# Sample values of a gated recurrence spread by DMA, and table products of a state-space layer in four row groups

## The chip, the cores and the metric

The kernel runs on one core of a Trainium2 chip. The metric is the device time of one execution in microseconds (us); the time before is the median of three runs. One further execution was profiled, and all rows come from it. Engines: TensorE (PE, its weight loads PEld), VectorE (DVE), ScalarE (ACT), GpSimd (POOL), SyncE (SP), which here only issues DMAs. All arithmetic is in 32-bit floats.

## The reference, cut to what matters

One step of a two-layer decoder trunk for a prompt of 512 tokens and 8 samples of one token each. Each layer is a half-step SwiGLU feed-forward block, a mixer, a cross-attention into 256 memory tokens and a second feed-forward block. Mixer 0 is S5, a diagonal complex state-space layer; mixer 1 is HGRN2, a gated recurrence with 8 heads and a 128x128 state per head. The change touches one piece of each.

For a sample, HGRN2 takes one step of the recurrence. Per head, with f, k, q and v vectors of 128:

```
S_new[k, v] = f[k] * S[k, v] + k_t[k] * v_t[v]        # 8 samples: 8 outer products
o[v]        = sum_k S_new[k, v] * q_t[k]
```

The kernel keeps channels on the 128 partitions: `k_t` of a sample is one column (a value per partition), which suits `f * S + k * v` with k on the partitions. But `v_t` also is a column, and the product needs it as a row that every partition can read.

For S5 the sequence is worked in blocks of 8 tokens. Tables hold the response of a group's 16 outputs to 16 inputs at 0 to 7 steps: products of `c * lambda^n` (`sGe` in the code) with `b` (`bZ`), summed over the 64 complex states of a group, plus the direct term `d` at step 0. They depend on the weights alone and are made on the chip at the start.

## The kernel before, in words

The trunk is a list of matrix products ("streams") over the same 520 token columns: for each pair of 128-column weight chunks, SP loads the chunk (`raw`), ScalarE rounds it (`w_hi`, L1329), VectorE takes the remainder (`w_lo`, L1826), and TensorE runs three products (`w_hi` with the high and low part of the activations, L3017, and `w_lo` with the high part, L3022). There are two `raw` buffers and two chunks (j = 0, 1) in a pair. SP issues a load when `lo_ready` says that VectorE has read the buffer's last content (L965). Each engine runs its own program in an order written out by hand; the engines meet in semaphores only.

S5 tables (during layer 0's first feed-forward block). GpSimd builds, for a = 0 to 7, the tables `sFe` and `sGe` of four pairs of groups (`table_part`, L736 to L738; `s5_tables` counts them). `sGe` has two buffers. At fixed places in its stream of products (`PREP`), TensorE's `prepare` runs two groups of transposes ("F") and then the group "K": for each of four pairs u, two products over bZ (real and imaginary part, 32 rows of output by 128 columns, L2565) and one of 16 columns with the identity (L2568). All four u write the PSUM partitions 0 to 31, at columns u*128. A 32-bit product is two instructions in the trace, a transpose one, so a "K" is 16 and 8 of them. ScalarE copies the bank to `sKst` (L1466) when the earlier table's copies have landed (`s5_k_out`), and SP writes it with 8 DMAs to memory (L945), each repeated over 8 steps. Places for a = 0 to 3 lie in `ffn1_out0` (one pair of chunks apart), for a = 4 to 7 in `ffn1_in1` (two pairs apart).

HGRN2 (`hg_in`, 16 pairs, two per head). The iteration h runs four weight chunks (forget gate, queries, values, output gate), and between them small groups for head g = h - 1 (attention inside chunks of 64 tokens, the state's increments "D", the outputs "O") and e = h - 2 (the samples' outputs "S" and "T", the norm "N", "R"). `HG` lists the groups in order; group q uses PSUM bank q mod 4, and TensorE waits for the bank's earlier content to be read (`reuse`). After "D" come two groups "B": TensorE transposes each sample's value column, repeated over 128 columns, against the identity (8 transposes per head, L2818), so that every partition holds the row v. VectorE reads it from PSUM: 8 instructions `sS = vrow * k + sS` (L2315), four per bank, after ScalarE has multiplied sS by f (L1703). VectorE's order in an iteration ends: values into `hgV` (L2187), the prompt's states (L2205), the samples' states (L2315), the split of the next pair's chunk 0 (L1826), two products (L2326, L2327), the output gate (L2329). SP loads the samples' states (L921, after the odd pair's loads), and stores those of head h - 2 (L908, L910, after the even pair's loads, from the fifth pair on). The weights of the next stream, `hg_out`, are requested by SP when the 16 pairs of `hg_in` are through; TensorE starts on them in iteration 8 (`projected`, L2896).

## Time and profile before

| what | value |
|---|---|
| median of 3 runs | 2366.99 us (2365.1 to 2368.97) |
| profiled execution, its own time | 2364.88 us |
| profiled execution, span | 2363.1 us |
| TensorE busy | 2341.2 us (99%) |
| VectorE, ScalarE, GpSimd busy | 1292.9, 871.4, 608.2 us |
| memory traffic | 289 MB, 122 GB/s on average |

The span is from the first to the last instruction; the execution's own time is 1.8 us more. Busy time of TensorE is the union of its matmuls, whose ends are modelled and overlap, so the cost of a group is best read as the distance from its start to the next group's start. A timeline row gives the start in us, the length, engine, line, operation, output and inputs, how many instructions are merged, and in brackets the idle time before it with its releaser.

### The profile page before, as it was taken

How to read it: one execution, taken by the hardware profiler on the slowest of the kernel's cores; microseconds unless marked ns; L12 is line 12 of the kernel's file. 1: busy time of each engine (PE TensorE's matmuls, PEld its weight loads, DVE VectorE, ACT ScalarE, POOL GpSimd, SP SyncE). 2: the span in 40 equal slices, each digit the busy share in tenths (PEclk: the TensorE clock that was granted, in tenths of full speed). 3: DMA queues.
4: the chain of work that ended last, by engine and by line, in shares of the span. 5: the costliest groups of instructions: out<-in, count | busy, mean ns of one | idle time of the engine just before them, and what ended most of it. 6: DMA issues, size and time to landing. Idle time of an engine off the chain costs nothing.

```text
span 2363.1 us, 50146 instructions
## 1 busy us (share of the span) xinstructions
PE 2341.2 (99%) x21043; PEld 2280.2 (96%) x21043; DVE 1292.9 (55%) x1906; ACT 871.4 (37%) x1399; POOL 608.2 (26%) x591
## 2 busy tenths in 40 slices
PE   8999999999999999999999999999999999999999
PEld 8999999889979999999999999999999979999999
DVE  6653643864576543445543344577778666443443
ACT  4422333543233231232333233267775233321323
POOL 4779958331103000004121010432222102000003
PEclk9999999999999999999999999999999999999999
DMA  6456445563463333333543333333332653333332
GB/s 169 128 156 151 119 123 156 182 184 107 148 242 101 95 91 91 98 104 87 169 119 106 105 104 116 86 99 103 109 104 81 214 188 90 98 94 94 98 93 95
DMA packets 483707, 289.19 MB, mean 122 GB/s; under 512 B 22289, under 2 KB 466962, under 8 KB 482514
## 3 DMA queue, kind: packets, MB, share of 16 engines
q1 hardware_dynamic: 477856, 280.66, 40.3%
q0 software_dynamic: 560, 1.84, 0.6%
q10 hardware_dynamic: 5122, 4.25, 0.5%
q8 instruction: 129, 2.11, 0.4%
q14 instruction: 40, 0.33, 0.0%
HBM read 258.86 MB, written 27.85 MB: 121 GB/s over the span
## 4 chain that ended last, share of the span: by engine, by line
PE 89%; DVE 4%; POOL 3%; ACT 2%; DMA 1%; issue 1%; SPq 0%; DVEq 0%; POOLq 0%; ACTq 0%
PE lin L3017 50%; PE lin L3022 25%; PE mis L2511 3%; POOL sTmp L737 1%; PE mis L2648 1%; PE mis L2631 1%; POOL sGe L738 1%; PE lin L2598 1%; POOL sGe L736 1%; PE lin L2979 1%; POOL sFe L738 1%; PE lin L2648 0%; DMA raw<-in_xattn_w_kv_dram 0%; PE lin L2760 0%; DVE w_lo L1826 0%
## 5 line engine op out<-in xcount | busy, mean ns | idle before, releaser
L1826 DVE TENSOR_TENSOR w_lo<-raw,w_hi 128x1024 fp32r<-128x1024 f32 (+1 forms) x322 | 463.4, 1439 | 297.7 <-ACT w_hi L1329 297.1
L1329 ACT ACTIVATE w_hi<-raw 128x1024 fp32r<-128x1024 f32 (+1 forms) x328 | 364.9, 1113 | 305.7 <-PE lin L3022 251.3
L3017 PE MATMUL lin<-a_rear,w_hi 128*128 128x264 f32 x3552 | 455.5, 279 | 0.0
L3017 PE MATMUL lin<-a_front,w_hi 128*128 128x256 f32 x3552 | 451.5, 279 | 1.1 <-DVE a_rear L1839 0.7
L3017 PEld LDWEIGHTS lin<-a_rear,w_hi 128*128 128x128 f32 x3552 | 432.6, 188 | 0.0
L3017 PEld LDWEIGHTS lin<-a_front,w_hi 128*128 128x128 f32 x3552 | 424.4, 188 | 4.6 <-issue 1.9
L3022 PE MATMUL lin<-a_rear,w_lo 128*128 128x264 f32 x1776 | 245.2, 278 | 0.0
L3022 PE MATMUL lin<-a_front,w_lo 128*128 128x256 f32 x1776 | 240.5, 277 | 0.9 <-DVE w_lo L1826 0.9
L2390 DVE SCALAR_TENSOR_TENSOR xT<-lin,xT 128x520 f32<-128x520 f32 (+1 forms) x87 | 60.8, 699 | 322.2 <-PE lin L3022 321.5
L1062 POOL TENSOR_TENSOR acc<-xT 128x520 f32<-128x520 f32 x8 | 12.2, 1520 | 864.0 <-DVE xT L2390 835.9
L3022 PEld LDWEIGHTS lin<-a_rear,w_lo 128*128 128x128 f32 x1776 | 223.8, 188 | 0.0
L3022 PEld LDWEIGHTS lin<-a_front,w_lo 128*128 128x128 f32 x1776 | 219.5, 188 | 1.6 <-DVE w_lo L1826 1.5
L1740 ACT ACTIVATE f_front<-t 128x256 fp32r<-128x256 f32 (+1 forms) x88 | 36.9, 419 | 395.1 <-DVE t L2371 395.1
L3017 PE MATMUL lin<-f_rear,w_hi 128*128 128x264 f32 x1386 | 178.1, 281 | 0.0
L3017 PEld LDWEIGHTS lin<-f_rear,w_hi 128*128 128x128 f32 x1386 | 170.5, 188 | 0.1
L3017 PE MATMUL lin<-f_front,w_hi 128*128 128x256 f32 x1386 | 170.3, 276 | 0.0
L3017 PEld LDWEIGHTS lin<-f_front,w_hi 128*128 128x128 f32 x1386 | 163.3, 188 | 0.1
L1736 ACT ACTIVATE t<-t 128x520 f32<-128x520 f32 x88 | 56.5, 642 | 278.6 <-DVE t L2365 278.6
L2369 DVE TENSOR_TENSOR t<-lin,rstd 128x520 f32<-128x520 f32 x88 | 61.5, 699 | 158.5 <-PE lin L3022 158.4
L1066 POOL TENSOR_TENSOR sqt<-xT 128x520 f32 (+1 forms) x54 | 81.9, 1517 | 211.0 <-DVE xT L2390 148.9
L3017 PE MATMUL lin<-g_all,w_hi 128*128 128x264 f32 (+1 forms) x1024 | 128.8, 278 | 0.0
L3017 PEld LDWEIGHTS lin<-g_all,w_hi 128*128 128x128 f32 x1024 | 122.8, 188 | 1.1 <-DVE g_all L1966 1.1
(512 smaller groups left out, 3207.9 us busy)
## 6 DMA issues: line engine op xcount, KB each, us to landing
raw<-in_ffn_w_in_dram SPq DMA_DIRECT2D x176, 512.0 KB, 3.9
raw<-in_ffn_w_out_dram SPq DMA_DIRECT2D x64, 704.0 KB, 4.6
kc<-in_cache_mem_k_dram SPq DMA_DIRECT2D x32, 512.0 KB, 7.0
vc<-in_cache_mem_v_dram SPq DMA_DIRECT2D x16, 1024.0 KB, 9.4
raw<-in_hg_w_in_dram SPq DMA_DIRECT2D x32, 512.0 KB, 4.3
raw<-in_xattn_w_kv_dram SPq DMA_DIRECT2D x16, 512.0 KB, 4.4
raw<-in_s_w_glu_dram SPq DMA_DIRECT2D x16, 512.0 KB, 4.1
raw<-in_xattn_w_q_dram SPq DMA_DIRECT2D x16, 512.0 KB, 3.9
```

The costliest lines, as they stand in the source:

```text
L736: link(eng.tensor_tensor(out[:, e], pv[0], mv[e], ALU.mult))
L738: link(eng.tensor_tensor(out[:, e], out[:, e], tmp, sign))
L1066: step.link(pool.tensor_tensor(sqt[:], tile(xT, m), tile(xT, m), ALU.mult))
L1329: act.activation(w_hi[:, j, 0:kt, :], raw[:, j, 0:kt, :], ACT.Copy).then_inc(hi_ready, 1)
L1736: act.activation(t2[:], t1[:], ACT.Silu).then_inc(gate_out, 1)
L1740: ins = act.activation(tile(out, i), t3[:, cols], ACT.Copy)
L1826: dve.tensor_tensor(low_weights(n, j), raw[:, j, 0:kt, :], w_hi[:, j, 0:kt, :].bitcast(F32), ALU.subtract).then_inc(lo_ready, 1)
L2369: step.link(dve.tensor_tensor(t4[:], lflat(1), rstd[:], ALU.mult))
L2390: dve.scalar_tensor_tensor(out=tile(xT, m), in0=lflat(j), scalar=scale, in1=tile(xT, m), op0=ALU.mult, op1=ALU.add)\
L2511: ins = pe.matmul(kv_bank(c)[:, 0:NM], w[:, e, k, :], x[:, k, :], start=k == 0 and u == 0, stop=k == KD - 1 and u == 2)
L3017: pe.matmul(lpart(j, half), high[:, k, :], (x_lo if u else x_hi)[half][:, k, :], start=start and u == 0 and k == 0, stop=False)
L3022: ins = pe.matmul(lpart(j, half), low[:, k, :], x_hi[half][:, k, :], start=False, stop=k == kt - 1)
```

## The change

"B" goes. TensorE's 16 groups (64 transposes) are left out of `HG` and of its program. In their place SP writes the head's 8 value columns from `hgV` to a small tensor in memory (`values_out`; the order is turned, so the pieces are 4 bytes, 1024 of them) and, in a second DMA, reads the 8 rows back into all 128 partitions (`values_spread`, 4 KB per partition, 512 KB in all) into `vB`, which has two buffers. VectorE takes the row from `vB` in SBUF instead of PSUM and waits for `spread_in`. A semaphore `sampled` takes the place of the old bank counters. In SP's program, with i the pair, `values_out(i // 2 - 1)` stands after the even pair's loads and `values_spread(i // 2 - 1)` after the odd pair's `sample_states_in`. `values_out` of the last head stands behind the loop, ahead of the first load of `hg_out`; its spread stands between the first pair's two loads.

"K" is packed. The four u write the PSUM partitions 32u to 32u+31, columns 0 to 127, with the loop over real and imaginary part outside; the four identity products follow. ScalarE then copies 128x128 instead of 32x512, and SP takes the rows from there.

```diff
+    vB = [at(f"vB{e}", [P, NS, P], F32, (o_hid + 6 * HTILE, o_tmp + 5 * TILE)[e]) for e in range(2)]
+    hg_v = nc.dram_tensor("hg_v", (HH, NS, P), F32, kind="Internal").ap()
...
-    sKst = at("sKst", [2 * SC, 4, P], F32, o_s0 + 31360)
+    sKst = at("sKst", [P, P], F32, o_s0 + 31360)
...
-            made += [("D", (g, 0), "dve"), ("D", (g, 1), "dve"), ("B", (g, 0), "dve"), ("B", (g, 1), "dve")]
+            made += [("D", (g, 0), "dve"), ("D", (g, 1), "dve")]
...
-                HG.emptied_of(sp, "B", (h, 1))
+                sp.wait_ge(sampled, h + 1)
                 sp.dma_start(o_["hg_s"][0, :, h].rearrange("b k v -> k b v"), sS[h % 2][:]).then_inc(hg["s_out"], 16)
+
+            def values_out(h):
+                sp.wait_ge(used[0], first_pair["hg_in", 1] + 2 * h + 2)
+                sp.dma_start(hg_v[h].rearrange("b v -> v b"), hgV[h % 2][:, SEQ:NT],
+                             allow_slow_non_contiguous=True).then_inc(spread_out, 16)
+
+            def values_spread(h):
+                sp.wait_ge(spread_out, 16 * (h + 1))
+                if h >= 2:
+                    sp.wait_ge(sampled, h - 1)
+                    sp.wait_ge(spread_in, 16 * h)
+                src = bass.AP(tensor=hg_v.tensor, offset=h * NS * P, ap=[[0, P], [P, NS], [1, P]])
+                sp.dma_start(vB[h % 2][:], src).then_inc(spread_in, 16)
...
-                            sp.dma_start(dst, sKst[SC * g:SC * (g + 1), u:u + 1, :].to_broadcast([SC, CS, P]))\
+                            r0 = 2 * SC * u + SC * g
+                            sp.dma_start(dst, sKst[r0:r0 + SC, :].unsqueeze(1).to_broadcast([SC, CS, P]))\
...
+                        if first and j == 0 and ST[n][0] == "hg_out":
+                            values_spread(HH - 1)
...
                         if i % 2:
                             sample_states_in(i // 2)
-                        elif i >= 4:
-                            states(i // 2 - 2)
+                            if i >= 3:
+                                values_spread(i // 2 - 1)
+                        elif i >= 2:
+                            values_out(i // 2 - 1)
+                            if i >= 4:
+                                states(i // 2 - 2)
+                    values_out(HH - 1)
...
-                        act.activation(sKst[:], bank[0:2 * SC, :].rearrange("p (j n) -> p j n", j=4), ACT.Copy)\
+                        act.activation(sKst[:], bank[:, 0:P], ACT.Copy)\
...
                 def values(p, b):
                     dve.wait_ge(chunk_done, 2 * p + 3)
+                    if p >= p0 + 4:
+                        dve.wait_ge(spread_out, 16 * ((p - p0) // 2 - 1))
...
+                        dve.wait_ge(spread_in, 16 * (g + 1))
                         for f in range(2):
-                            q = G.at("B", (g, f))
                             dve.wait_ge(hg["s_decay"], 2 * g + f + 1)
-                            dve.wait_ge(hg["fill"], q + 1)
                             for u in range(4):
                                 s_ = 4 * f + u
                                 ins = dve.scalar_tensor_tensor(
-                                    out=sS[g % 2][:, s_], in0=hg_bank(q)[:, u * P:(u + 1) * P],
+                                    out=sS[g % 2][:, s_], in0=vB[g % 2][:, s_],
                                     scalar=hgK[g % 2][:, SEQ + s_:SEQ + s_ + 1], in1=sS[g % 2][:, s_],
                                     op0=ALU.mult, op1=ALU.add)
-                            ins.then_inc(hg["void_dve"], 1)
+                        ins.then_inc(sampled, 1)
...
+                        rows = [slice(2 * SC * u, 2 * SC * (u + 1)) for u in range(4)]
+                        for e in range(2):
+                            for u in range(4):
+                                pe.matmul(bank[rows[u], 0:P], bZ[:, e, 4 * a + u, :, :].rearrange("p g c -> p (g c)"),
+                                          sGe[a % 2][:, e, u, 0:CS, :], start=e == 0, stop=False, skip_group_check=True)
                         for u in range(4):
-                            for e in range(2):
-                                pe.matmul(bank[0:2 * SC, u * P:(u + 1) * P],
-                                          bZ[:, e, 4 * a + u, :, :].rearrange("p g c -> p (g c)"),
-                                          sGe[a % 2][:, e, u, 0:CS, :], start=e == 0, stop=False)
-                            ins = pe.matmul(bank[0:2 * SC, u * P:u * P + SC], ident[:, 2 * SC * u:2 * SC * (u + 1)],
-                                            dD[:, a, :], start=False, stop=True)
+                            ins = pe.matmul(bank[rows[u], 0:SC], ident[:, rows[u]], dD[:, a, :], start=False, stop=True,
+                                            skip_group_check=True)
...
-                elif what == "B":
-                    h, f = a
-                    for u in range(4):
-                        b = SEQ + 4 * f + u
-                        ins = pe.transpose(bank[:, u * P:(u + 1) * P], hgV[h % 2][:, b:b + 1].to_broadcast([P, P]), ident[:])
...
                         hg_increments(g)
-                        hg_group("B", (g, 0))
-                        hg_group("B", (g, 1))
```

Left out of the diff: the semaphores' declarations, and three waits on "B" (ScalarE before it overwrites `hgK`, TensorE before "S", SP above) that now name `sampled`.

## Rows read from the trace of the kernel before

**Rows 1.** The page: busy us and share; TensorE's granted clock in 40 slices.

```profile
PE 2341.2 (99%) x21043; PEld 2280.2 (96%) x21043; DVE 1292.9 (55%) x1906; ACT 871.4 (37%) x1399; POOL 608.2 (26%) x591
...
PEclk9999999999999999999999999999999999999999
```

**Rows 2.** Stretches, one head: length, busy PE, PEld, DVE, ACT, POOL, clock, DMA share, GB/s.

```profile
1649.00:1681.00 32.00, 32.00 (x368) 30.41 (x367) 24.34 (x50) 23.58 (x39) 7.59 (x8) 1.00 0.37 102
```

**Rows 3.** Timeline of TensorE, first table group: start, duration, what.

```profile
157.70 0.62 PE L2565 MATMUL mis<-sGe,bZ 128*32 128x128 f32 x4
158.16 0.21 PE L2568 MATMUL mis<-dD,ident 128*32 128x16 f32 x2
...
159.80 2.39 PE L3017 MATMUL lin<-f_rear,w_hi 128*128 128x264 f32 x18
```

**Rows 4.** The same view of TensorE, a steady head.

```profile
1635.27 0.64 PE L2784 MATMUL mis<-sS,hgQ 128*32 128x128 f32 x16
1635.84 0.66 PE L2798 MATMUL mis<-ident,hgV 128*128 128x128 f32 x4
...
1652.22 1.09 PE L2818 MATMUL mis<-ident,hgV 128*128 128x128 f32 x8
1653.07 2.13 PE L3017 MATMUL lin<-a_front,w_hi 128*128 128x256 f32 x16
```

**Rows 5.** Timeline of GpSimd, ends of the third, fourth and fifth table.

```profile
192.80 1.43 POOL L738 TENSOR_TENSOR sGe<-sGe,sTmp 128x576 f32<-128x576 f32 x1
...
212.00 1.41 POOL L738 TENSOR_TENSOR sGe<-sGe,sTmp 128x576 f32<-128x576 f32 x1
...
231.34 2.29 POOL L738 TENSOR_TENSOR sGe<-sGe,sTmp 128x576 f32<-128x576 f32 x1
```

**Rows 6.** Timeline of TensorE at the third, fourth and fifth table.

```profile
194.56 0.62 PE L2565 MATMUL mis<-sGe,bZ 128*32 128x128 f32 x4
...
213.60 0.60 PE L2565 MATMUL mis<-sGe,bZ 128*32 128x128 f32 x4 [0.54 <-POOLq L1190]
...
239.11 0.62 PE L2565 MATMUL mis<-sGe,bZ 128*32 128x128 f32 x4
```

**Rows 7.** Timeline of VectorE: two products and a sample update.

```profile
1569.01 1.23 DVE L2326 TENSOR_TENSOR dgQ<-dgQ,hgQ 128x512 f32<-128x512 f32 x1 [0.62 <-ACT dgQ L1696]
...
1657.45 2.15 DVE L2315 SCALAR_TENSOR_TENSOR sS<-mis,hgK,sS 128x128 f32<-128x128 f32 x8
...
1660.66 0.68 DVE L2326 TENSOR_TENSOR dgQ<-dgQ,hgQ 128x512 f32<-128x512 f32 x1
```

**Rows 8.** Timeline of TensorE in the second head's span.

```profile
1599.25 0.97 PE L3022 MATMUL lin<-a_front,w_lo 128*128 128x256 f32 x6 [0.45 <-DVE w_lo L1826]
```

**Rows 9.** Timeline of SyncE's queue at the end of the stage.

```profile
1770.22 10.53 SPq L965 DMA_DIRECT2D raw<-in_hg_w_out_dram  x2
```

**Rows 10.** Timeline of VectorE there.

```profile
1782.11 0.69 DVE L2187 TENSOR_TENSOR hgV<-lin,rstd 128x520 f32<-128x520 f32 x1
...
1787.72 1.22 DVE L1826 TENSOR_TENSOR w_lo<-raw,w_hi 128x1024 fp32r<-128x1024 f32 x1
...
1801.87 2.06 DVE L2315 SCALAR_TENSOR_TENSOR sS<-mis,hgK,sS 128x128 f32<-128x128 f32 x8
```

**Rows 11.** Timeline of ScalarE there.

```profile
1784.99 1.05 ACT L1329 ACTIVATE w_hi<-raw 128x1024 fp32r<-128x1024 f32 x1
```

**Rows 12.** Timeline of TensorE there.

```profile
1789.77 0.39 PE L2896 MATMUL lin<-h_hi,w_hi 128*128 128x256 f32 x1
...
1791.75 0.65 PE L2784 MATMUL mis<-sS,hgQ 128*32 128x128 f32 x16 [0.28 <-ACT hO L1718]
...
1804.04 0.72 PE L2874 MATMUL mis<-rT,ident 64*128 64x130 f32 x8 [0.15 <-DVE sS L2315]
```

**Rows 13.** The page's DMA issues: pieces' tile, KB each, median us to landing.

```profile
raw<-in_hg_w_out_dram SPq DMA_DIRECT2D x8, 512.0 KB, 3.8
...
bRaw<-in_s_b_re_dram SPq DMA_DIRECT2D x2, 128.0 KB, 5.4
```

More of the change, by code:

```diff
@@ L453, in trunk_kernel @@
            "scaled_dve", "front", "state_out", "s_decay", "s_out", "squares", "inverse")}
-    rows_in = [sem(f"rows_in{b}") for b in range(NS)]
+    rows_in = [sem(f"rows_in{b}") for b in range(4)]
+    spread_out, spread_in, sampled = sem("spread_out"), sem("spread_in"), sem("sampled")
     consts_done = sem("consts_done")
@@ L1646, in hg_in @@
                         if h >= 2:
-                            G.emptied_of(act, "B", (h - 2, 1))
+                            act.wait_ge(sampled, h - 1)
                             act.wait_ge(hg["scaled_pool"], POOLS * (h - 1))
@@ L2780, in hg_group @@
                 if what == "S":
-                    G.emptied_of(pe, "B", (a, 1))
+                    pe.wait_ge(sampled, a + 1)
                     for b in range(NS):
```

## The prediction

> **What bounds the kernel now.** I read the page first. TensorE is busy for 2341.2 of 2363.1 us and its clock is granted in full in all 40 slices, so the upper of the two levels throughout [rows 1]. No other engine is above 55%. So the span is TensorE's program, with some 22 us of gaps, and what leaves TensorE's program shortens the span unless another engine is late at the next meeting. Then I read the two stages that the change touches. In a steady head of the HGRN stage TensorE works 32.00 of 32.00 us, VectorE 24.34, ScalarE 23.58 [rows 2]. In the table stage TensorE's groups stand close behind GpSimd's tables: the fourth "K" is the one place where TensorE waits for them, 0.54 us [rows 6].
>
> **K packed.** Before, a group lasts from 157.70 to 159.80, 2.10 us; one u has a quarter, 0.525 us; its two small instructions start 0.46 us after its four large ones, so a large one costs 0.115 us and a small one (0.525 - 0.46)/2 = 0.03 us [rows 3]. How the packed form runs is shown by the "S" groups: the same shape (128 rows, 32 columns of weights, 128 moving columns) in turns over four sets of output partitions, and 16 instructions from 1635.27 to 1635.84, 0.036 us each [rows 4]. So a new K is 16 x 0.036 + 8 x 0.036 = 0.86 us, and saves 1.24 us. The bounds: nothing, if only "S" overlaps for a reason of its own, and 2.10 - 0.57 = 1.53 us if the small ones hide. I take 1.24, from the nearest row.
>
> The Trainium skill (TensorE: Matmul & The Clock Gate, "The mechanism") states that a weight load overlaps running matmuls only when it is for other rows of the array; here all groups use all 128 rows, so by that rule the packed K would save nothing. The "S" rows, also on 128 rows, speak against it; what it would give is the second rival.
>
> How many of the eight count? GpSimd's third and fourth sGe end at 194.23 and 213.41; TensorE takes them at 194.56 and 213.60 [rows 5, 6]. GpSimd works without regard to when TensorE is done. When the first two K save 2.48 us, TensorE stands at the third at 192.08 and waits until 194.4; the fourth starts at 213.6 as before. So the savings of the first three are all given back as waits, and only the fourth's own 1.24 us is left. The fifth table ends at 233.63 and is used at 239.11, 5.5 us of slack; that place is 25.5 us behind the fourth's, the later ones as far apart again, where a table takes 20 us [rows 5, 6], so the last four save in full (a wait of ScalarE for the earlier copies' landing stands in the same stretch and moves with them). K: 5 x 1.24 = 6.2 us. The smaller copy on ScalarE is off the path.
>
> **B removed.** From the start of "B" to the next chunk is 1653.07 - 1652.22 = 0.85 us, 6.8 us over eight heads [rows 4]. In the five middle heads (g = 1 to 5) nothing is late behind it: the chunk of weights between hides VectorE's work, and both helpers are idle for some 8 us in 32 [rows 2]. They save 4.25 us. The first head (g = 0) saves nothing: TensorE already waits 0.45 us for a split that stands behind the sample update in VectorE's program [rows 8], and comes 0.85 us earlier to the same wait. For the last two see below.
>
> **What VectorE pays.** An update takes 2.06 to 2.15 us for eight, 0.26 us each, from PSUM [rows 7, 10]. From SBUF both inputs share a memory with GpSimd's work. A product of 512 columns takes 0.68 us alone and 1.23 us beside GpSimd [rows 7], so the streaming part of 0.13 us of a 128-column one can double; against that the read from PSUM goes. I take +0.3 us for eight with GpSimd at work (bounds: -0.5 and, with all of it doubled, +2.1). It counts only in the first head, where the split is waited for: -0.3 us. In middle heads it is hidden.
>
> **The DMAs.** The spread of head g is issued behind the sample states' load, which waits for the end of "S" at 1635.84 [rows 4], so at about 1636.5; 512 KB land in 3.8 us alone [rows 13], at most some 9 us behind the states' load. VectorE wants them at 1657.45 [rows 7]: over 10 us of slack. The turned store is 1024 pieces of 4 bytes, 64 per DMA engine. The trace has no such store. Nearest is bRaw: 2048 pieces of 64 bytes landing in 5.4 us behind another load [rows 13], hence at most 0.04 us per piece and engine. I take 0.01 to 0.04 us, 1 to 3 us for all 64 and landing in 2 to 4 us; as bounds nothing and 0.2 us a piece. The DMAs are busy for 0.37 of a head [rows 2] and SP has pauses where the two stand.
>
> The Trainium skill (DMA: Bandwidth & Descriptors, "Rules for kernel authors") states that a copy whose last dimension isn't contiguous becomes one descriptor per element, and the same page, "Specifications", that pieces below 512 bytes cost a read-modify-write. No row here shows what that makes of a 4-byte store; its effect would be the fourth rival.
>
> **The end of the stage is where the change costs.** SP requested `hg_out`'s first chunk at 1770.22 and its second ten us later [rows 9]. Now `values_out(7)` stands ahead of them and waits for hgV of head 7, which ends at 1782.80 [rows 10]. So the first load starts at 1783.35 instead of 1770.22 and lands after 3.8 us [rows 13], at 1787.15; ScalarE, which split it at 1784.99 [rows 11], now does so from 1787.2 to 1788.25, and VectorE's split, before from 1787.72 to 1788.94 [rows 10], ends at 1789.5. TensorE's first product of `hg_out` was at 1789.77 [rows 12]; without B it would be there at 1788.9 and waits until 1789.55. Behind the split stand the output gate and ScalarE's copy of "O", for which TensorE already waits at 1791.75 [rows 12]; that meeting moves by the split's delay, 0.57 us. So the seventh head's saving (g = 6) is gone, and 0.6 us are lost. The second load must wait for the store's landing, about 1785, and arrives near 1790.2, ahead of its use, which follows the copies of "O" at 1792 [rows 12]. With the store at its 4 us both shift and the loss is 2 to 4 us. In the last head (g = 7) TensorE waits in "R" for a bank that the update frees [rows 12]; now "R" takes a bank that is free, but "S" behind it needs the update, which ends at 1803.93 [rows 10] against 1803.8 for TensorE: some 0.6 of the 0.85 us stay.
>
> **Sum.** 6.2 + 4.25 - 0.3 - 0.6 + 0.6 = 10.15 us. The profiled execution's own time is 1.8 us above its span: 2364.9 - 10.15 = 2354.7 us. The median shown stands 2.1 us above that execution: 2366.99 - 10.15 = 2356.8 us. The likeliest case's own range is 2354 to 2360 (updates at +0.3 or below, store of 1 to 3 us).
>
> **Rivals.**
> 1. GpSimd doesn't hold TensorE. If its tables came sooner, for instance because the freed TensorE or VectorE gets out of its way, all eight K count: 3 x 1.24 = 3.7 us more, and the two ends of HGRN without loss another 2.5: 2366.99 - 16.4 = 2350.6 us. Against it: its table ends are set by its own unbroken work [rows 5].
> 2. The packed K runs no faster: 2366.99 - 3.95 = 2363.0 us. For it only that weights and moving columns differ from "S" in content; against it the 0.036 us [rows 4].
> 3. HGRN gives nothing: store at 4 us and update at +1 us, so 3 us at the end and 1 us in the first head against 4.25 + 0.6: 2366.99 - 6.2 - 0.85 = 2359.9 us, or up to 2362 if ScalarE's long wait moves too.
> 4. Slower, by SP's queue: the 4-byte pieces take 0.2 us each. Then the 64 of an engine last 12.8 us, `hg_out`'s first chunk lands at 1786.2 + 12.8 = 1799.0, 12.4 us late for VectorE; in six middle heads the next weights arrive about 1.8 us after they are wanted, 10.8 us. Against 10.8 us saved elsewhere that is 12.4 us slower: 2379.4 us. It decides from about 0.17 us a piece. For it: no row shows such a store, and waits of SP and VectorE now hang on it. Against it: 64-byte pieces at 0.04 us or less [rows 13].
>
> **How the numbers follow.** A difference counts above 0.2% (4.7 us), about what this kernel's measurement can tell from none; so faster means below 2362.3. Chances: forecast 0.55, rival 1 0.08, rival 2 0.12, rival 3 0.17, rival 4 0.08. Faster: 0.55 + 0.08 + 0.14 of rival 3 + 0.02 of rival 2 = 0.79; slower 0.08; same 0.13. The range leaves out rival 4 and most of rival 1 and reaches over rival 2: 2352.5 to 2364.0.
>
> **What would show it.** Right: L2565 in about 0.6 us a group of 16, next chunk 0.86 us after its start; TensorE's wait on GpSimd up from 0.5 to about 4 us in two waits; no L2818; about 31.2 us a head; `hg_out`'s first load some 13 us after its old place in the head and a wait of TensorE near its first product. Wrong: a K still near 2 us (rival 2); the third and fourth K without waits (rival 1); L2315 above 3 us, or VectorE waiting for `spread_in` (3, 4); landings of the 4-byte store above 5 us. The forecast as a whole is wrong if TensorE's gaps grow by more than what left its program.

## The result, and the profile after

The changed kernel takes 2375.68 us, median of 11 runs (2371.62 to 2376.94), against 2367.34 us for 11 runs of the kernel before on the same chips. The ratio is 1.0033, 95% interval 1.0025 to 1.0041: about 8 us slower, where 10 us less were forecast and 2364.0 was the range's end. The profiled execution took 2376.84 us, its span is 2375.1 us.

The page of the changed kernel, the lines that answer to [rows 1]:

```profile
PE 2335.1 (98%) x20979; PEld 2271.5 (96%) x20979; DVE 1305.3 (55%) x1906; ACT 870.4 (37%) x1399; POOL 605.0 (25%) x591
...
PEclk9999999999999999999999999999998999999999
```

TensorE's work fell by only 6.1 us, and its gaps grew from 22 to 40 us: by the prediction's last sentence that alone makes it wrong. One slice of the clock is no longer full. The list of TensorE's waits in the changed kernel (line waited at, releaser: total us, times, longest) says where:

```profile
PE lin L2920 <- DVE w_lo L1853: 11.0, 1, 11.0
...
PE lin L3044 <- DVE w_lo L1853: 3.8, 4, 2.9
PE mis L2594 <- POOLq L1217: 3.0, 2, 2.8
...
PE mis L2839 <- ACT vTok L1663: 1.7, 1, 1.7
```

**The stage's end.** The queue of SyncE, then ScalarE, VectorE and TensorE in the changed kernel, the answer to [rows 9 to 12]:

```profile
1782.41 0.37 SPq L919 DMA_DIRECT2D hg_v<-hgV  x1
1782.83 0.57 SPq L985 DMA_DIRECT2D raw<-in_hg_w_out_dram  x1
1792.69 0.33 SPq L929 DMA_DIRECT2D vB<-hg_v  x1
...
1797.05 1.06 ACT L1356 ACTIVATE w_hi<-raw 128x1024 fp32r<-128x1024 f32 x1 [12.39 <-DMA raw<-in_hg_w_out_dram]
...
1787.75 0.72 PE L2898 MATMUL mis<-rT,ident 64*128 64x130 f32 x8
1799.42 0.58 PE L2920 MATMUL lin<-h_hi,w_hi 128*128 128x256 f32 x1 [10.96 <-DVE w_lo L1853]
1799.80 0.41 PE L2920 MATMUL lin<-h_lo,w_hi 128*128 128x256 f32 x1
1800.01 0.41 PE L2920 MATMUL lin<-h_hi,w_lo 128*128 128x256 f32 x1
...
1802.32 1.08 PE L2813 MATMUL mis<-sS,hgQ 128*32 128x128 f32 x16
```

The store of 4-byte pieces is requested at 1782.41; the spread, which waits for nothing but its landing, follows at 1792.69, 10.3 us later. The load of weights behind it is in memory 14.2 us after its request, where such a load took 3.8 [rows 13]. And once TensorE has stood for 11 us, its products start 0.21 us apart instead of 0.12, and "S" takes 1.08 us instead of 0.65 [rows 12]: the lower of the two clock levels. The view by stretches (length, busy PE, PEld, DVE, ACT, POOL, granted clock, DMA share, GB/s) shows how long that lasts:

```profile
1799.40:1805.40 6.00, 5.98 (x40) 5.00 (x41) 4.38 (x7) 3.18 (x8) 0.00 (x0) 0.50 0.39 113
1800.00:1820.00 20.00, 18.89 (x246) 16.24 (x246) 14.11 (x35) 11.55 (x25) 0.00 (x0) 0.86 0.19 55
```

A granted clock of 0.50 is the lower level throughout: some 6 us of work at half speed, so about 3 us lost.

The slow store doesn't show as busy DMA engines. The DMA view of the stretch from 1782 to 1784.8 counts the packets; two rows of the view by stretches follow:

```profile
DMA packets 1072, 0.02 MB, mean 7 GB/s; under 512 B 1040, under 2 KB 1072, under 8 KB 1072
...
1784.80:1786.80 2.00, 2.00 (x27) 1.80 (x25) 1.91 (x4) 0.00 (x0) 2.00 (x2) 1.00 0.00 0
1786.80:1792.60 5.80, 1.66 (x38) 1.40 (x36) 1.90 (x7) 0.00 (x0) 0.18 (x1) 0.94 0.33 29
```

All 1024 pieces have started by 1784.8. For the next 2 us nothing moves, and up to the landing the load behind them trickles at 29 GB/s. What the time between the last piece's start and the landing goes into isn't shown.

**The second head.** It answers to [rows 8], where TensorE waited 0.45 us. SyncE, ScalarE, VectorE and TensorE of the changed kernel:

```profile
1561.47 0.37 SPq L919 DMA_DIRECT2D hg_v<-hgV  x1
1564.62 6.30 SPq L985 DMA_DIRECT2D raw<-in_hg_w_in_dram  x2
...
1576.95 1.06 ACT L1356 ACTIVATE w_hi<-raw 128x1024 fp32r<-128x1024 f32 x1 [6.62 <-DMA raw<-in_hg_w_in_dram]
...
1595.05 4.63 DVE L2343 SCALAR_TENSOR_TENSOR sS<-vB,hgK,sS 128x128 f32<-128x128 f32 x8
...
1578.55 0.66 PE L2839 MATMUL mis<-lvl 128*64 128x32 f32 x16 [1.75 <-ACT vTok L1663]
...
1579.65 3.30 PE L3039 MATMUL lin<-a_front,w_hi 128*128 128x256 f32 x16
...
1600.86 2.08 PE L3044 MATMUL lin<-a_front,w_lo 128*128 128x256 f32 x8 [2.89 <-DVE w_lo L1853]
```

Two things are late here: ScalarE's split of weights whose load stands behind the first head's store, with the copy vTok behind it; and VectorE's w_lo, behind an update of 4.63 us where it was 2.15 [rows 7]. After each wait a run of 16 products that takes 2.1 us takes 3.3, or eight take 2.08 instead of 1.07.

**K.** The first packed group, and the third, in the changed kernel, the answer to [rows 3, 6]:

```profile
159.44 0.64 PE L2594 MATMUL mis<-sGe,bZ 128*32 128x128 f32 x16
...
160.06 1.12 PE L3039 MATMUL lin<-f_rear,w_hi 128*128 128x264 f32 x7
...
196.33 0.65 PE L2594 MATMUL mis<-sGe,bZ 128*32 128x128 f32 x16 [2.84 <-POOLq L1217]
...
196.95 4.47 PE L3039 MATMUL lin<-f_rear,w_hi 128*128 128x264 f32 x22
```

A group costs 0.62 us, not 2.10. The wait on GpSimd's third table is the forecast one; the 22 products behind it take 4.47 us where such a run takes 2.78 elsewhere: again the lower clock, 1.7 us. That fall costs nothing in the end, because the fourth table isn't there any earlier. In a second profile of K packed alone (k_only_again) the clock stayed up, and TensorE waited for the fourth table instead:

```profile
194.56 0.64 PE L2567 MATMUL mis<-sGe,bZ 128*32 128x128 f32 x16 [2.85 <-POOLq L1191]
...
195.19 2.87 PE L3019 MATMUL lin<-f_rear,w_hi 128*128 128x264 f32 x22
...
213.73 0.64 PE L2567 MATMUL mis<-sGe,bZ 128*32 128x128 f32 x16 [2.14 <-POOLq L1191]
```

The wait there is 2.14 us; in the changed kernel it is 0.15.

For the comparisons below the HGRN stage is measured between events that every kernel has: VectorE's hgV of the first, third and eighth head, and the request of the first load of the stage after `hg_out`. From TensorE's first K group to the first scan product of the state-space stage is K's part. All in us, from one profiled execution each; the row of before is first:

| kernel | first K | K to scan | hgV 1 to 3 | hgV 3 to 8 | hgV 8 to end | HGRN sum |
|---|---|---|---|---|---|---|
| before | 157.70 | 267.88 | 57.52 | 161.23 | 54.50 | 273.25 |
| changed | 159.44 | 262.65 | 63.38 | 157.57 | 66.20 | 287.15 |
| k_only | 159.20 | 262.00 | 57.54 | 161.24 | 54.49 | 273.27 |
| hg_only | 162.61 | 267.85 | 63.63 | 159.35 | 65.32 | 288.30 |
| load_first | 160.11 | 262.08 | 64.46 | 157.61 | 55.10 | 277.17 |
| pieces32 | 159.42 | 261.91 | 62.25 | 160.61 | 56.61 | 279.47 |
| before_sbuf | 157.87 | 267.98 | 59.24 | 161.75 | 55.83 | 276.82 |
| no_transfers_k | 158.51 | 263.89 | 60.73 | 157.84 | 55.24 | 273.81 |
| k_late | 159.70 | 262.03 | 57.49 | 161.24 | 54.49 | 273.22 |
| mixed | 157.90 | 260.56 | 57.48 | 158.72 | 55.59 | 271.79 |
| mixed_again | 161.11 | 260.43 | 57.51 | 158.72 | 55.67 | 271.89 |
| k_only_again | 157.64 | 260.55 | 57.49 | 161.23 | 54.49 | 273.21 |
| mixed25 | 159.93 | 260.46 | 57.48 | 158.91 | 54.50 | 270.89 |

The opening scatters: the first K group stands anywhere from 157.6 to 162.6, which is why medians and not single spans are compared. The HGRN columns repeat to 0.1 us (mixed and mixed_again, k_only and k_only_again).

"K to scan" has two levels among the ten profiles with packed groups: 260.4 to 260.6 us in mixed, mixed_again, mixed25 and k_only_again, and 261.9 to 263.9 in the other six. In those six the clock fell around 416 us, just before the scan, for 3.4 us (no_transfers_k: 6.8), and in the four it didn't. k_only and k_only_again are the same program, so this is scatter between executions. A row of k_only, then the same stretch of k_only_again:

```profile
414.00:421.00 7.00, 6.55 (x52) 6.02 (x50) 5.42 (x10) 3.44 (x12) 2.36 (x1) 0.76 0.33 86
...
414.00:421.00 7.00, 7.00 (x120) 6.81 (x122) 5.99 (x12) 3.57 (x11) 1.03 (x1) 1.00 0.74 213
```

What makes it fall there isn't shown: TensorE's waits just before, 0.9 and 0.45 us, are the same in before, where it stays up (1.00 in this stretch).

### The profile page after: what moved, and what is told of

Its sections match the earlier page's. It is cut to its first block, busy times and chain, and to the rows that moved or that the text cites. A ratio compares the mean times of both kernels' runs of the same rounds, so it can differ in the third digit from the quotient of the medians.

```text
span 2375.1 us, 50038 instructions
## 1 busy us (share of the span) xinstructions
PE 2335.1 (98%) x20979; PEld 2271.5 (96%) x20979; DVE 1305.3 (55%) x1906; ACT 870.4 (37%) x1399; POOL 605.0 (25%) x591
## 4 chain that ended last, share of the span: by engine, by line
PE 70%; DVE 6%; ACT 3%; DMA 2%; issue 1%; POOL 0%; DVEq 0%; SPq 0%; ACTq 0%; POOLq 0%
PE lin L3039 40%; PE lin L3044 20%; PE mis L2539 3%; DVE sS L2343 1%; PE mis L2677 1%; PE mis L2660 1%; DVE w_lo L1853 1%; DMA raw<-in_hg_w_out_dram 1%; DVE hS L2234 1%; DMA raw<-in_hg_w_in_dram 1%; PE lin L2677 0%; DMA raw<-in_xattn_w_kv_dram 0%; PE lin L2789 0%; ACT w_hi L1356 0%; PE lin L2920 0%
```

## The experiments

**1. K alone (k_only).** The kernel before with the four edits of the K groups: the shape of `sKst`, the source rows of its stores, ScalarE's copy and the order of the products.

```
-    sKst = at("sKst", [2 * SC, 4, P], F32, o_s0 + 31360)
+    sKst = at("sKst", [P, P], F32, o_s0 + 31360)
...
+                                pe.matmul(bank[rows[u], 0:P], bZ[:, e, 4 * a + u, :, :]...
```

> The kernel before with the packed K groups alone; HGRN keeps its B transposes. Theory 1 (the loss is all HGRN's: the store of 4-byte pieces holds up the SyncE queue, and TensorE, once idle, works at the lower clock for some us; K packed keeps its gain): 0.62 us a group instead of 2.10 saves 1.48 each, 11.8 over eight, of which about 3 go into waits on GpSimd's tables at the third and fourth group and 1.5 to 2 into products at the lower clock behind the third: 4 to 7 us faster than before (about 2362). Rival A (packing K is what fails: the wait at the third table and the clock fall cost as much as the eight groups gain): within 1 us of before.

Measured: 2359.8 us, ratio 0.9968 (0.9956 to 0.998), 7.3 us faster, just above the 4 to 7 expected. Rival A is out. Its HGRN stage is that of before to 0.02 us.

**2. HGRN alone (hg_only).** All the other edits of the change, K groups as before.

> The kernel before with HGRN's two transfers alone; K groups as before. Theory 1: the wait of 11 us at the stage's end with 3 us of slow products behind it, and some 5 to 6 us in the second head, less about 0.6 us a head in five heads: 11 to 15 us slower than before. Rival A: 7 to 9 us slower, the whole of the change's loss. Rival B (the loss comes from VectorE's slower update of sS, whose operands now all lie in SBUF): the same total, but with waits of TensorE on VectorE in every head.

Measured: 2384.63 us, ratio 1.0072 (1.0058 to 1.0086), 17.5 us slower, beyond what was expected. The HGRN stage accounts for 15.05 us of it (in the profiled execution the opening was 4.9 us longer as well). The two halves of the change (-7.3 and +17.5) add up to the +8 within their intervals. Rival B's waits in every head aren't there: between the third and eighth hgV it is faster than before (159.35 and not 157.6, for one gap of 1.4 us that no wait explains).

**3. The load ahead of the store (load_first).**

```
-                        if first and j == 0 and ST[n][0] == "hg_out":
+                        if first and j == 1 and ST[n][0] == "hg_out":
+                            values_out(HH - 1)
                             values_spread(HH - 1)
...
-                    values_out(HH - 1)
                     return
```

> The changed kernel, with hg_out's first two weight loads issued ahead of the last head's store and spread; nothing else moved. Theory 1: hg_out's first load is in memory in time, TensorE's 11 us wait at 1799 and the slow products behind it go (about 13 us): 2361 to 2365 us, faster than before by 2 to 6; the last head's sample update comes later, but has the first hg_out chunks to hide in. Rival B: only the queue's part goes and VectorE still holds TensorE: 2366 to 2370.

Measured: 2365.68 us, ratio 0.9993 (0.9983 to 1.0002): 10 us less than the changed kernel, between theory 1's 2365 and rival B's 2366. The profile decides between them. The first `hg_out` product in this kernel, and the store and spread:

```profile
1784.30 0.37 SPq L919 DMA_DIRECT2D hg_v<-hgV  x1
1795.46 0.34 SPq L929 DMA_DIRECT2D vB<-hg_v  x1
...
1791.79 0.38 PE L2920 MATMUL lin<-h_hi,w_hi 128*128 128x256 f32 x1 [1.44 <-DVE w_lo L1853]
1792.01 0.28 PE L2920 MATMUL lin<-h_lo,w_hi 128*128 128x256 f32 x1
```

The store still takes 11 us, but nothing waits for it. The wait of 10.96 is 1.44, the products come 0.12 apart, and the last stretch falls from 66.20 to 55.10. So it is the load's place behind the slow store, the order on SyncE's queue, that cost 11 us. The 0.6 us that remain at the end and the 6.9 in the first heads have other causes (experiments 5 and 6).

**4. Pieces of 32 bytes (pieces32).** The changed kernel; DRAM holds the values as [v][b], and VectorE strides.

```
-                sp.dma_start(hg_v[h].rearrange("b v -> v b"), hgV[h % 2][:, SEQ:NT],
-                             allow_slow_non_contiguous=True).then_inc(spread_out, 16)
+                sp.dma_start(hg_v[h], hgV[h % 2][:, SEQ:NT]).then_inc(spread_out, 16)
...
-                                    out=sS[g % 2][:, s_], in0=vB[g % 2][:, s_],
+                                    out=sS[g % 2][:, s_], in0=vB[g % 2][:, :, s_],
```

> The changed kernel, but the eight sample values of a partition are stored as one piece of 32 bytes (128 pieces instead of 1024), the spread stays one contiguous read of 4096 bytes per partition, and VectorE reads its values with a stride of 32 bytes. The order on the SyncE queue is that of the change. Theory 1 (price per piece, about 0.15 us for each of 64 on a DMA engine): the store lands 2 to 3 us after its issue instead of 10, and hg_out's first load 4 to 7 us instead of 14: 2360 to 2365 us, and the second head's wait goes too. Rival C (the price is the write through memory itself or its order in the queue, not the number of pieces): the store still lands 8 to 10 us after issue and the time stays at 2374 to 2377. Strided reads on VectorE: none of the theories needs them slower; if they are, the update takes over 4 us for eight in every head.

Measured: 2367.64 us, ratio 0.9998 (0.9989 to 1.0007). The queue of SyncE, and VectorE in a steady head:

```profile
1783.58 0.34 SPq L919 DMA_DIRECT2D hg_v<-hgV  x1
1783.97 0.43 SPq L984 DMA_DIRECT2D raw<-in_hg_w_out_dram  x1
1784.99 0.32 SPq L928 DMA_DIRECT2D vB<-hg_v  x1
...
1658.32 4.07 DVE L2342 SCALAR_TENSOR_TENSOR sS<-vB,hgK,sS 128x128 f32<-128x128 f32 x8
```

The same 4 KB, through the same memory and in the same place of the queue, have landed after 1.4 us as 128 pieces (8 per DMA engine) and after 10.3 us as 1024 (64): (10.3 - 1.4)/56 = 0.16 us a piece and engine. This is a quotient of landing times; by the packets above no engine is seen to work 0.16 us on a piece. Rival C is out, and the wait on vTok is gone too. The edit also changes which pieces lie side by side in memory (neighbouring 4-byte pieces of the turned store come from different partitions); that this, and not the count, makes the store slow was not tested. The total missed its forecast: the strided read makes the update 4.07 instead of 3.45 us, a steady head lasts 32.0 us as before the change, and TensorE still waits 3.49 us for w_lo in the second head and 1.97 at the first `hg_out` product. What removing B and packing K give is eaten by VectorE.

**5. Only the operand's place (before_sbuf).** The kernel before; VectorE reads the identity tile instead of the bank, TensorE still makes B.

```
-                                    out=sS[g % 2][:, s_], in0=hg_bank(q)[:, u * P:(u + 1) * P],
+                                    out=sS[g % 2][:, s_], in0=ident[:],
```

> The kernel before, whose only edit is that VectorE's sS update reads the identity tile in SBUF instead of the sample values in PSUM (the new states are wrong by that; TensorE still makes and VectorE still awaits the B groups, no transfer is added). It tells what makes an update of eight take 3.5 us in the steady heads and 4.6 us in the first instead of 2.15. Theory 2 (an operation with both tile operands in SBUF is slower while GpSimd works): 3.4 to 3.5 us in the steady heads, over 4 in the first, 2.1 in the last head where GpSimd is idle, and TensorE waits about 3 us on w_lo in the second head: 3 to 5 us slower than before. Rival D (the new transfers' traffic makes it slower): 2.15 us everywhere, time as before.

Measured: 2371.45 us, ratio 1.0009 (1.0 to 1.0018), 3.0 us slower by the medians, and an HGRN stage 3.6 us longer. TensorE waits 2.08 us for w_lo in the second head, not the 3 expected. VectorE in a steady head and in the last head of this kernel:

```profile
1660.35 3.51 DVE L2315 SCALAR_TENSOR_TENSOR sS<-ident,hgK,sS 128x128 f32<-128x128 f32 x8
...
1806.63 2.09 DVE L2315 SCALAR_TENSOR_TENSOR sS<-ident,hgK,sS 128x128 f32<-128x128 f32 x8
```

No transfer is added here, so rival D is out: the operand's place alone takes the update from 2.15 to 3.51, and in the last head, where GpSimd is idle, it costs nothing. The way it happens shows in the changed kernel. Windows narrow enough to hold a single update, beside GpSimd's last two operations of that head:

```profile
1659.62 0.60 DVE L2343 SCALAR_TENSOR_TENSOR sS<-vB,hgK,sS 128x128 f32<-128x128 f32 x1
1660.15 1.35 DVE L2343 SCALAR_TENSOR_TENSOR sS<-vB,hgK,sS 128x128 f32<-128x128 f32 x1
...
1658.80 1.28 POOL L1322 TENSOR_TENSOR outK<-outK,hgK 128x512 f32<-128x512 f32 x1
1660.04 1.31 POOL L1324 TENSOR_TENSOR inQ<-inQ,hgQ 128x512 f32<-128x512 f32 x1
```

The group is not slower evenly. Six of the eight updates take their usual 0.34 us (starting 0.26 apart). The first begins while GpSimd's outK operation is under way and ends 0.15 us after it (1660.22 against 1660.07); the second begins 0.11 us into the next operation and ends 0.15 us after that one. The first two are held for 0.26 and 1.01 us, together the 1.3. The first head has three such holds, 0.39, 1.03 and 1.03 us, and so its group costs 2.5 us more:

```profile
1595.05 0.73 DVE L2343 SCALAR_TENSOR_TENSOR sS<-vB,hgK,sS 128x128 f32<-128x128 f32 x1
1595.70 1.37 DVE L2343 SCALAR_TENSOR_TENSOR sS<-vB,hgK,sS 128x128 f32<-128x128 f32 x1
1596.99 1.37 DVE L2343 SCALAR_TENSOR_TENSOR sS<-vB,hgK,sS 128x128 f32<-128x128 f32 x1
...
1594.88 0.75 POOL L1320 TENSOR_TENSOR lvl<-lvl,hgK 128x256 f32<-128x256 f32 x1
1595.56 1.36 POOL L1322 TENSOR_TENSOR outK<-outK,hgK 128x512 f32<-128x512 f32 x1
1596.88 1.34 POOL L1324 TENSOR_TENSOR inQ<-inQ,hgQ 128x512 f32<-128x512 f32 x1
```

The Trainium skill (SBUF — State Buffer, "Who interferes with whom") states that a VectorE instruction with two SBUF inputs and a GpSimd instruction that reads SBUF exclude each other, the later one blocked until the first is done. The trace agrees, 1.35 us against 1.31. It agrees without exception: in the profile of the changed kernel 15 of the 64 updates begin during a GpSimd operation, and each of them ends 0.15 us after it; the other 49 take at most 0.35 us.

**6. B removed, no transfers (no_transfers_k).** The changed kernel without store, spread and their waits; the update reads the identity tile.

```
-                            if i >= 3:
-                                values_spread(i // 2 - 1)
...
-                    values_out(HH - 1)
...
-                        dve.wait_ge(spread_in, 16 * (g + 1))
```

> The changed kernel without its two transfers: nothing is stored or spread, nobody waits for them, and the sS update reads the identity tile in SBUF (the new states are wrong by that). It shows what the removal of B is worth when the transfers cost nothing. By theory 2 a steady head is 31.4 us as in the changed kernel (not shorter), the second head's wait on w_lo stays, the waits at vTok and at the stage's end go: 2359 to 2362 us. Rival D: the w_lo wait goes as well, 2354 to 2357.

Measured: 2362.43 us, ratio 0.9977 (0.9967 to 0.9987), a stage of 273.81 us: even with free transfers, removing B and reading the row from SBUF makes the stage 0.56 us longer. Rival D is out here too. What makes this kernel faster than before is K packed. The steady stretch gains 3.4 us (161.23 to 157.84); the first heads lose 3.2, the end 0.7. TensorE in the second head of this kernel:

```profile
1597.97 1.69 PE L3034 MATMUL lin<-a_front,w_lo 128*128 128x256 f32 x8 [3.05 <-DVE w_lo L1846]
1599.46 3.19 PE L3029 MATMUL lin<-a_rear,w_hi 128*128 128x264 f32 x16
```

The transfers themselves cost nothing in steady heads (157.57 with them), 2.7 to 3.7 us in the first, and 11 at the end.

**7. K packed from the fourth group on (k_late).**

```
+K_LATE = 3
...
+                        for e in range(2) if a >= K_LATE else ():
```

> The kernel before with K packed for the fourth to eighth group alone. If the first three packed groups only win time that GpSimd's third table and the lower clock behind that wait take back (3 x 1.48 = 4.4 us won, 2.8 waited, about 1.7 at the lower clock), this is as fast as all eight packed: 2359 to 2361 us, and TensorE has no wait over 1 us before 400. Rival E (the wait is not paid for by the first three groups, or the clock's fall costs nothing): all eight packed stay ahead of it by over 1.5 us.

Measured: 2360.74 us, ratio 0.9966 (0.9954 to 0.9978), and 262.03 us from the first K group to the scan, against 262.00 with all eight packed (k_only; the clock fell around 416 us in both, so they compare). The first three packed groups are worth nothing, as the prediction had it. But for the input at the opening, no single wait before the scan is above 0.9 us.

**8. Spread only where it pays (mixed, mixed_again, mixed25).** All K groups packed; the heads outside the list keep B.

```
+SPREAD = list(range(2, 7))        # mixed; range(2, 6) in mixed25
...
+            if g not in SPREAD:
+                made += [("B", (g, 0), "dve"), ("B", (g, 1), "dve")]
```

> All K groups packed; HGRN's values spread by the two transfers only for the third to seventh of the eight heads, the first two and the last keep their B transposes. By theories 1 and 2 it has the 0.64 us of each steady head (5 heads, 3.2 us) without the second head's waits and without the store ahead of hg_out's first load: 3 us faster than K packed alone, 2355 to 2358. Rival F (the transfers cost as much in the steady heads as B): no faster than K packed alone, 2359 to 2361.

Measured: 2362.46 us (2356.17 to 2366.62), ratio 0.9978 (0.9969 to 0.9987), slower than expected (2355 to 2358) though its stage is 1.5 us shorter than k_only's. So it was repeated beside k_only, with mixed25:

> The mixed version again, beside K packed alone on the same chip: its median was 2362.5 where its profiled execution gave 2356. If that is the scatter of the opening (TensorE's first table group stood between 157.7 and 162.6 us in the profiles so far, whatever the kernel), the median is 2358 to 2362 and the stage's length again 271.8 +- 0.3. If the transfers disturb in some executions, the stage of this profile is over 1 us longer.

> K packed alone, again, as the mate of the two mixed versions: 2359 to 2361 us, stage 273.3 us.

> As the mixed version, but with the transfers only for the third to sixth head (4 heads; the first two and the last two keep B). In the mixed version the stage was 1.5 us shorter than with all B groups, and not 3.2: the seventh head's update (3.5 us) delays w_lo for hg_out's first chunk (TensorE waits 1.43) and hO (1.05 instead of 0.28), 1.9 us more than before. Theory 2: with B in the seventh head both waits go back to those of before, the stage is 4 x 0.64 = 2.6 us shorter than 273.3 (270.7), and the time 2 to 3 us under K packed alone: 2357 to 2358. Rival F: the stage is no shorter than 271.8 and the time within 1 us of K packed alone.

Measured: mixed_again 2360.25 us (0.9954 to 0.9978), k_only_again 2360.17 (0.9948 to 0.9975), mixed25 2357.95 (0.9943 to 0.997). The run mixed_again is thus no faster than k_only_again, though its stage is 1.3 us shorter; its opening was 3.5 us later (161.11 against 157.64 in the profiles). mixed25 lies within what was expected of it. The stage of mixed25 is 270.89 us, 2.4 shorter than before, and its `hg_out` products are reached without the wait on w_lo. With the seventh head's row from SBUF (mixed) the same place showed 1.43 us of waiting, and it did so in no_transfers_k, where nothing is stored: that wait is VectorE's longer update. TensorE there in mixed25, the answer to the middle one of [rows 12]:

```profile
1783.35 0.64 PE L2836 MATMUL mis<-sS,hgQ 128*32 128x128 f32 x16 [0.25 <-ACT hO L1760]
```

mixed25 is the fastest of all, 11 us (0.43%) under the kernel before. Its lead of 2.2 us over K packed alone is what its stage shows, but within the scatter of the medians; by the runs' times alone it isn't settled.

## Why the prediction was wrong, step by step

- **K packed** held. The group saves 1.48 us, not 1.24, near the upper bound of 1.53: the large instructions cost 0.029 us each and the small ones about 0.02, not 0.036. The savings of the first three are given back, and k_late shows it by itself. In k_only_again they are given back as waits of 2.85 and 2.14 us; in the changed kernel as 2.84 and 0.15 and 1.7 at the lower clock between the two. What had no term is the other fall of the clock, around 416 us, in six of the ten profiles with packed groups: "K to scan" is 7.3 us shorter than before without it (5 x 1.48 = 7.4) and 4.0 to 6.0 with it. Measured for K alone -7.3 us against -6.2. Rival 2 is out, and so is the rule of the Trainium skill behind it (TensorE: Matmul & The Clock Gate, "The mechanism"): K packed runs as "S" does, although each group uses all rows of the array.
- **B removed** was mis-sized: 3.4 us over five steady heads in no_transfers_k, 0.68 each, where 0.85 was taken. "Nothing is late behind it" was wrong by 0.24 us in each of the last four (32.05 us a head became 31.44); 0.10 to 0.16 of it shows as TensorE's wait for the bank that VectorE's hO empties behind the longer update.
- **What VectorE pays** failed. Taken: +0.3 us for eight, one head. Measured: +1.3 in a steady head and +2.5 in the first, where it counts in full; the second figure is outside even the bound of +2.1. The error is the model: I let the streaming part double, and the measured form is that an update which begins during a GpSimd operation stands still until that is over. With the clock's fall behind it, the first heads lose 3.2 us without any transfer (57.52 to 60.73), where the prediction counted 0.3.
- **The DMAs** failed on the size. Taken: 0.01 to 0.04 us a piece, landing in 2 to 4 us. Measured: 0.16, landing in 10.3. The nearest row, 64-byte pieces, was no guide to 4-byte ones. The Trainium skill's rule of one descriptor per element (DMA: Bandwidth & Descriptors, "Rules for kernel authors") would have made the count of pieces the thing to fear. Its rule on pieces below 512 bytes (the same page, "Specifications") doesn't tell these cases apart, since 32-byte pieces landed in 1.4 us.
- **The end of the stage** had the right mechanism and the wrong size. The load did start 12.6 us later than [rows 9], and everything named behind it was late; but the last stretch grew by 11.7 us (54.50 to 66.20), where the sum had -0.6 for the end and +0.6 for the last head. It follows from the step before: the load's delay by a slow store, plus some 3 us of products at the lower clock. Of the 11.7, 0.7 come without any store, from the held update of the seventh head (55.24 in no_transfers_k).
- **The sum** of the profiled pair: K -5.2, first heads +5.9, steady heads -3.7, end +11.7, opening +1.7, all else +1.6, together +12.0 us of span. The medians differ by 8.3: the profiled execution of before lies 2.5 us under its median (its opening, 157.70, is one of the shortest), that of the changed kernel 1.2 above.
- **Rival 4** (chance 0.08) named the cause at the end and was close in its price, 0.2 us a piece for 0.16. It said that it decides from 0.17, so it was short where the other two costs were missing, and its 10.8 us in the middle heads didn't come: those heads aren't hurt by the transfers at all. That its total of 2379.4 us lies only 3.7 from the measured 2375.68 is in part luck: the 10.8 us were missing, and the loss in the first heads and at the lower clock wasn't in it.

Left open: why the stretch between the scan and the HGRN stage was up to 2 us longer than before in some profiles, with the transfers (hg_only, load_first) and without them (before_sbuf, k_only_again); why the clock falls around 416 us in some executions; and what holds the 4-byte store after its last piece has started.

## What to carry to other kernels

Before a transposing store goes on a queue, count its pieces per DMA engine and look at what stands behind it; move the next load ahead of it, or write whole short rows. Replacing a PSUM operand by one in SBUF isn't free on VectorE: look at what GpSimd does at that moment, and add what is left of each of its operations that an update meets, not a share of it. Where the bounding engine comes to stand for some us, add the slow products behind the wait to the price of the wait, unless its next wait takes them in; and apply a change that works in the steady state to the steady state alone.

## What the runs showed of the hardware

- A store of 64 pieces of 4 bytes per DMA engine has landed after 10.3 us, 0.16 us a piece; eight 32-byte pieces per engine have landed within 1.4 us. All the 4-byte pieces had started 2.4 us after the request, and the DMA engines' share was 0.00 in the 2 us that followed. A load requested 0.4 us behind 64 such pieces per engine was there after 14.2 us instead of 3.8.
- Matmuls with 32 columns of weights and 128 moving columns, in turns over four sets of output partitions, start 0.029 us apart (16 in 0.46 us), with float32 and all 128 rows in use; in one set they needed 0.115 us.
- Two waits of TensorE that were followed by products at the lower clock: after 2.84 us, 22 in 4.47 us instead of 2.78; after 1.75 us, 16 in 3.30 instead of 2.1. Waits alone don't tell: after 2.85 us in k_only_again 22 products took 2.87 us, at full speed, and so did those behind the wait of 1.44 us in load_first, with 1.05 soon behind it.
- A VectorE update with both tile operands in SBUF that began during a GpSimd operation ended 0.15 us after it, in all 15 cases of the changed kernel (0.60 to 1.37 us long), and took 0.34 us otherwise; with one operand in PSUM all eight took 0.34 us beside the same GpSimd work.
- A strided read (32 bytes between elements) of one operand made eight updates 0.6 us longer (4.07 against 3.45), and in the last head, without GpSimd, 2.81 against 2.09.
